# First norm in fewer steps, three start tiles on TensorE, norm tiles scaled ahead, and new places for the first chunks' second pieces

## The reference

```
def _modulate(h, shift, scale):
    return _rms(h) * (1.0 + scale) + shift

def _swiglu(h, w13, w2):
    a, b = jnp.split(h @ w13, 2, axis=-1)
    return (jax.nn.silu(a) * b) @ w2
...
    ml = _split_mod(cond_lat @ mod_w[i] + mod_b[i])
    mc = _split_mod(cond_ctx @ mod_w[i] + mod_b[i])
    h = h + 0.5 * ml[2] * _swiglu(_modulate(h, ml[0], ml[1]), ffn1_w13[i], ffn1_w2[i])
    hc = hc + 0.5 * mc[2] * _swiglu(_modulate(hc, mc[0], mc[1]), ffn1_w13[i], ffn1_w2[i])
```

## Time and profile before

| what | us |
|---|---|
| median of 3 runs | 1986.03 |
| lowest, highest | 1985.92, 1988.64 |
| profiled execution | 1990.15 |
| its span | 1988.5 |
| TensorE busy in it | 1927.3 |
| VectorE, ScalarE, GpSimd busy | 1149.1, 656.8, 156.7 |

### The profile page before, as it was taken

The page is one execution under the profiler, slowest core; times in us unless marked ns, Lnnn a source line. Parts: engine busy times, 40 slices in busy tenths (PEclk is TensorE's granted clock), DMA queues, the critical chain, the costliest instruction groups (busy, mean ns, idle before and its releaser), DMA issues.

```text
span 1988.5 us, 29548 instructions
## 1 busy us (share of the span) xinstructions
PE 1927.3 (97%) x11036; PEld 1695.6 (85%) x11036; DVE 1149.1 (58%) x1888; ACT 656.8 (33%) x1028; POOL 156.7 (8%) x212
## 2 busy tenths in 40 slices
PE   8899999999988899999999999999989999999998
PEld 7788888898965688888889888888888999999998
DVE  3887773345468558777533887752362532755554
ACT  2323222233236433322222423232243322544443
POOL 1210100100001211010010100100100000010000
PEclk9799999999989899999999999999999999999999
DMA  7365652234210036566332566633333220554554
GB/s 286 116 207 185 199 188 88 89 113 153 85 64 1 1 106 199 183 198 197 121 101 81 181 196 194 197 108 102 101 128 118 87 86 16 164 175 150 187 161 137
DMA packets 81004, 270.86 MB, mean 136 GB/s; under 512 B 8992, under 2 KB 14368, under 8 KB 80800
## 3 DMA queue, kind: packets, MB, share of 16 engines
q1 hardware_dynamic: 62496, 202.69, 31.3%
q0 software_dynamic: 18432, 67.12, 11.0%
HBM read 268.72 MB, written 1.05 MB: 136 GB/s over the span
## 4 chain that ended last, share of the span: by engine, by line
PE 91%; DVE 5%; issue 1%; ACT 1%; DMA 0%; POOL 0%; POOLq 0%; DVEq 0%; SPq 0%; ACTq 0%
PE pt L1167 22%; PE pt L1168 22%; PE pt L1170 22%; PE pt L1266 2%; PE pt L1375 2%; PE pt L1376 2%; PE pt L1374 2%; PE pt L1512 2%; PE pt L1514 2%; PE pt L1513 2%; PE pt L1458 1%; PE pt L1270 1%; DVE wl L735 1%; PE pt L1410 1%; PE pt L1391 1%
## 5 line engine op out<-in xcount | busy, mean ns | idle before, releaser
L735 DVE TENSOR_TENSOR wl<-raw,wh 128x1024 fp32r<-128x1024 f32 (+2 forms) x396 | 434.8, 1137 | 531.5 <-ACT wh L521 527.9
L1167 PE MATMUL pt<-xh,wh 128*128 128x512 f32 (+1 forms) x1648 | 595.0, 361 | 6.9 <-DVE wl L735 6.9
L1168 PE MATMUL pt<-xh,wl 128*128 128x512 f32 (+1 forms) x1648 | 594.0, 360 | 0.0
L1170 PE MATMUL pt<-xl,wh 128*128 128x512 f32 (+1 forms) x1648 | 592.2, 360 | 0.0
L521 ACT CAST wh<-raw 128x1024 fp32r<-128x1024 f32 (+2 forms) x396 | 366.0, 971 | 242.9 <-PE pt L1170 186.1
L1167 PEld LDWEIGHTS pt<-xh,wh 128*128 128x128 f32 x1648 | 313.0, 190 | 53.4 <-DVE wl L735 4.1
L1168 PEld LDWEIGHTS pt<-xh,wl 128*128 128x128 f32 x1648 | 312.9, 190 | 45.6
L1170 PEld LDWEIGHTS pt<-xl,wh 128*128 128x128 f32 x1648 | 312.7, 190 | 45.5
L747 DVE CUSTOM_DVE_ANT_0 pt<-modw,raw 128x1024 f32<-128x1024 f32 x256 | 305.7, 1256 | 5.0 <-DMA modw<-in_mod_rows 4.8
L1170 PE MATMUL pt<-ul,wh 128*128 128x512 f32 (+1 forms) x572 | 204.2, 357 | 0.0
L1167 PE MATMUL pt<-uh,wh 128*128 128x512 f32 (+1 forms) x572 | 204.2, 357 | 0.0
(11 more groups left out here) (169 smaller groups left out, 2355.3 us busy)
## 6 DMA issues: line engine op xcount, KB each, us to landing
raw<-in_ffn_w SPq DMA_DIRECT2D x240, 512.0 KB, 4.0
modw<-in_mod_rows POOLq DMA_DIRECT2D x128, 512.0 KB, 4.6
raw<-in_ret_w_in SPq DMA_DIRECT2D x48, 512.0 KB, 4.4
raw<-in_diff_w_in SPq DMA_DIRECT2D x24, 512.0 KB, 4.5
raw<-in_ffn_w SPq DMA_DIRECT2D x32, 256.0 KB, 3.9
raw<-in_ret_w_out SPq DMA_DIRECT2D x16, 512.0 KB, 4.2
region<-in_mod_start SPq DMA_DIRECT2D x9, 512.0 KB, 9.2
raw<-in_ffn_w SPq DMA_DIRECT2D x32, 128.0 KB, 3.4
```

Source lines behind the costliest of these rows:

```text
L735: nc.vector.tensor_tensor(flat(wl[:, s, cut]), raw[:, raw_slot(late, s, p), 0:part_rows * CW], flat(wh[:, s, cut].bitcast(F32)), ALU.subtr ...
L1167: nc.tensor.matmul(bank, wh[:, s, k, cut], hi(k), start=a, stop=False)
L1168: nc.tensor.matmul(bank, wl[:, s, k, cut], hi(k), start=False, stop=False)
L1170: return nc.tensor.matmul(bank, wh[:, s, k, cut], lo(k), start=False, stop=b)
```

## The change

There are four parts.

1. START_PE_SCALES is 3 instead of 1: TensorE makes the scale tiles of columns 0, 1 and 2, all ahead of the broadcast.
2. The second pieces of the first two chunks are loaded into the two modw slots. SyncE waits for nothing there, the pieces have semaphores of their own, ScalarE and VectorE read them from modw, and `raw_count` no longer counts the first pieces. GpSimd's first fetch into modw waits until both have been subtracted (lo_ready 4); it no longer stands behind any xl.
3. In norm 0 VectorE makes one scaled tile in two halves (hT times sc1 times the root), ScalarE adds the shift and rounds, and VectorE makes xl of tile k - 1 after the scaled tile of k (`start_lo`). GpSimd's xl step is gone, and tmp has four slots in turn.
4. In the later norms VectorE makes four scaled tiles (two in the second half) before the first xl, and keeps that lead. The two rests come at k = 0 and 2 (2 and 4). Ahead of ret_q the first copy_out with its cast, and the rest, stand before the second half's tiles; the second ones are at k = 3.

```diff
-START_PE_SCALES = 1
+START_PE_SCALES = 3
...
         def rests_among(ph):
-            return {4: {2: [(16, 0)], 4: [(16, 1)], DT: [(17, 0)], DT + 1: [(17, 1)]}, 2: {-1: [(9, 0), (9, 1)]},
-                    1: {4: [(5, 0)], 6: [(5, 1)]}}[len(ph["rows"])]
+            return {4: {0: [(16, 0)], 2: [(16, 1)], DT: [(17, 0)], DT + 1: [(17, 1)]}, 2: {-1: [(9, 0), (9, 1)]},
+                    1: {2: [(5, 0)], 4: [(5, 1)]}}[len(ph["rows"])]
...
             def start_pieces(p):
+
                 for s in range(2):
-                    if p:
-                        sp.wait_ge(lo_ready, s + 1)
-                    sp.dma_start(raw[:, s, :], column(w13[1][0], s * UP_PAIRS, p * DT // 2, DT // 2)).then_inc(raw_landed[s], 16)
+                    where = modw_slot[:, s] if p else raw[:, s, :]
+                    sp.dma_start(where, column(w13[1][0], s * UP_PAIRS, p * DT // 2, DT // 2)).then_inc(start_piece_landed[2 * p + s], 16)
...
-                    for k in range(DT):
-                        pool.wait_ge(affine, 2 * (k + 1))
-                        pool.wait_ge(x_hi_done, 2 * (k + 1))
-                        nc.gpsimd.tensor_tensor(xl[:, k, :], tmp[:, 2 + k % 2, :], xh[:, k, :].bitcast(F32),
-                                                ALU.subtract).then_inc(x_ready, 1)
...
+                    if u0 == START_UNITS:
+
+                        pool.wait_ge(lo_ready, 4)
...
-                                nc.scalar.activation(xh[:, k, cut], tmp[:, k % 2, cut], ACT.Identity, bias=modT[:, m0 + k, b:b + 1],
-                                                     scale=sc1[:, k, b:b + 1]).then_inc(x_hi_done, 1)
+                                nc.scalar.activation(xh[:, k, cut], tmp[:, k % 4, cut], ACT.Identity,
+                                                     bias=modT[:, k, b:b + 1]).then_inc(x_hi_done, 1)
...
+                        if after["kind"] == "ret_q":
+                            copy_out(after, qr, LAT, 0, 0)
                         for k in range(DT):
                             half_tile(1, k)
-                            if after["kind"] == "ret_q" and k % 4 == 3:
-                                copy_out(after, qr, LAT, 0, k // 4)
+                            if after["kind"] == "ret_q" and k == 3:
+                                copy_out(after, qr, LAT, 0, 1)
...
+                    def start_lo(k):
+                        for b in range(2):
+                            cut = slice(b * LAT, (b + 1) * LAT)
+                            dve.wait_ge(x_hi_done, 2 * k + b + 1)
+                            ins = nc.vector.scalar_tensor_tensor(xl[:, k, cut], tmp[:, k % 4, cut], modT[:, k, b:b + 1],
+                                                                 xh[:, k, cut].bitcast(F32), ALU.add, ALU.subtract)
+                        ins.then_inc(x_ready, 1)
...
-                        if k >= 2:
-                            dve.wait_ge(x_hi_done, 2 * (k - 1))
-                        nc.vector.tensor_tensor(tmp[:, k % 2, :], hT[:, k, :], pt[:, BC, :], ALU.mult).then_inc(normed, 1)
-                        dve.wait_ge(normed, k + 1)
-                        if k >= 2:
-                            dve.wait_ge(x_ready, k - 1)
+                        if k >= 4:
+                            dve.wait_ge(x_ready, k - 3)
                         for b in range(2):
                             cut = slice(b * LAT, (b + 1) * LAT)
-                            nc.vector.tensor_scalar(tmp[:, 2 + k % 2, cut], tmp[:, k % 2, cut], sc1[:, k, b:b + 1],
-                                                    modT[:, k, b:b + 1], ALU.mult, ALU.add).then_inc(affine, 1)
+                            ins = nc.vector.scalar_tensor_tensor(tmp[:, k % 4, cut], hT[:, k, cut], sc1[:, k, b:b + 1],
+                                                                 pt[:, BC, cut], ALU.mult, ALU.mult)
+                        ins.then_inc(normed, 1)
+                        if k:
+                            start_lo(k - 1)
+                    start_lo(DT - 1)
...
+                    for k in range(4):
+                        scaled_tile(0, k)
                     for k in range(DT):
                         rests(k)
-                        scaled_tile(0, k)
-                        if k:
-                            x_lo(0, k - 1)
-                    x_lo(0, DT - 1)
+                        x_lo(0, k)
+                        if k + 4 < DT:
+                            scaled_tile(0, k + 4)
...
+                        if after["kind"] == "ret_q":
+                            rest(2 * (after["q"] + 1), 0, late=is_late(after))
                         dve.wait_ge(bcast_ready, ph["st"] + 2)
+                        for k in range(2):
+                            scaled_tile(1, k)
                         for k in range(DT):
```

More of the change, by code:

```diff
@@ L263, in trunk @@
         x_hi_done = sem("x_hi_done")
-        normed, affine = sem("normed"), sem("affine")
+        normed = sem("normed")
         sq_ready, sq_added = sem("sq_ready"), sem("sq_added")
@@ L273, in trunk @@
         x_landed = [sem(f"x_landed{g}") for g in range(4)]
+        start_piece_landed = [sem(f"start_piece_landed{n}") for n in range(4)]
         start_made, start_step, start_cols = sem("start_made"), sem("start_step"), sem("start_cols")
@@ L359, in raw_count @@
             if not late:
-                return 2 * pair + s + 1
-            return pair - late_pair + 1 + (2 * late_pair if s == 0 else 0)
+                return 2 * pair + s - 1
+            return pair - late_pair + 1 + (2 * late_pair - 2 if s == 0 else 0)
         def is_late(ph):
@@ L561, in start_pieces @@
                 for s in range(2):
-                    act.wait_ge(raw_landed[s], 16 * (p + 1))
-                    nc.scalar.copy(flat(wh[:, s, p * DT // 2:(p + 1) * DT // 2]), raw[:, s, :]).then_inc(hi_ready, 1)
+                    cut = slice(p * DT // 2, (p + 1) * DT // 2)
+                    act.wait_ge(start_piece_landed[2 * p + s], 16)
+                    nc.scalar.copy(flat(wh[:, s, cut]), modw_slot[:, s] if p else raw[:, s, :]).then_inc(hi_ready, 1)
             act.wait_ge(cols_landed, 16)
@@ L741, in start_pieces @@
                     dve.wait_ge(hi_ready, 2 * p + s + 1)
-                    nc.vector.tensor_tensor(flat(wl[:, s, cut]), raw[:, s, :], flat(wh[:, s, cut].bitcast(F32)),
-                                            ALU.subtract).then_inc(lo_ready, 1)
+                    nc.vector.tensor_tensor(flat(wl[:, s, cut]), modw_slot[:, s] if p else raw[:, s, :],
+                                            flat(wh[:, s, cut].bitcast(F32)), ALU.subtract).then_inc(lo_ready, 1)
             def column_sum(dst, weights, j, products):
@@ L946, in _ @@
                     if T == TOK:
+                        if after["kind"] == "ret_q":
+                            rest(2 * (after["q"] + 1), 0, late=is_late(after))
                         dve.wait_ge(bcast_ready, ph["st"] + 2)
+                        for k in range(2):
+                            scaled_tile(1, k)
                         for k in range(DT):
-                            scaled_tile(1, k)
-                            if k:
-                                x_lo(1, k - 1)
-                            if k == DT - 1:
-                                x_lo(1, k)
-                            if after["kind"] == "ret_q" and k % 4 == 3:
-                                rest(2 * (after["q"] + 1) + k // 4, k // 4, late=is_late(after))
+                            x_lo(1, k)
+                            if k + 2 < DT:
+                                scaled_tile(1, k + 2)
+                            if after["kind"] == "ret_q" and k == 3:
+                                rest(2 * (after["q"] + 1) + 1, 1, late=is_late(after))
                     if units_of(L, first + 2) <= ph["unit"] - START_UNITS:
```

## The result

The changed kernel takes 2001.94 us (median of 4 runs, 1999.85 to 2005.69), against 1987.34 for the kernel before (4 runs, 1985.92 to 1990.4). The medians differ by 14.6 us. The ratio is 1.0068, 95% interval 1.0052 to 1.0084, which of 1987.34 is 13.5 us, 10 to 17: slower. The forecast was 1996.4, range 1986 to 2006, slower with 0.78.

A forecast was written before the change was run, and what follows sets the result against it. TensorE was taken to bound the kernel, so only its waits in the start and norms count. Start +21.7 and norms -11.3 gave +10.4, put on 1986.0 rather than the profiled 1990.15: 1996.4 us, range 1986 to 2006.

The forecast's parts named there:

- The head, +7.0: Start: two more scale tiles ahead of the broadcast delay S1, the end of column 1's shift tile on TensorE, by 7.0 us.
- S1 to S3, +0.4: Start, from column 1's shift tile end to column 3's: first turn unchanged, second 5.0 us against 4.56, so +0.4.
- S3 to S7, +13.3: Start, shift tile ends of columns 3 to 7: TensorE and VectorE take turns, three of four at 1.2 GHz, 40.0 us, +13.3.
- S7 to the end, +1.0: Start, from column 7's shift tile end to the last product: -0.5 at the high clock, +2.6 at the low, taken as +1.0.
- Behind it nothing changes: Behind the start: cast, small part and first loop pair follow the start's end as before, so no further change.
- The norms, -11.3: Later norms: 4.65 from three norms at 1.55 each, 0.25 at 722, 3.94 and 2.5 at ret_q; bounds -14.5 to -6.
- 1.37 plus the 0.51 of the pause in front: Norms at 417, 1085 and 1452: these TensorE waits go, less 0.3 for the moved piece, some 1.55 us each.
- The norm at 722: Norm with one chunk: moving both rests two tiles ahead shifts its 2.0 us of pauses rather than removing them, gaining 0.25.
- ret_q: Behind the norm at 1452: TensorE's 3.94 us wait for the next chunk's small part goes, and the high clock gives 2.5.
- (1): Start: the clock stays high or falls no more than before, +1.9 in all, 1987.9 us, no change told; chance 0.14.
- (2): Start: memory path freed of GpSimd decides, VectorE's sums set the old turn, -8.2 with the norms, 1977.8 us; chance 0.08.
- (3): Norms give nothing because the rests at k = 0 hold up xl: +21.7, 2007.7 us; chance 0.06.

The follow-up runs named there:

- e11: The kernel before with part 1 alone, three scale tiles on TensorE ahead of the broadcast: 1996.71 us, ratio 1.0036 to the kernel before.
- e4: The changed kernel with xl of tile k made right behind its scaled tile, ahead of the columns of k+1: 1986.05 us, ratio 0.9981 to the kernel before.
- e1: The kernel before with part 4 (the norms) alone: 1978.47 us, ratio 0.995 to the kernel before.
- e10: The kernel before with part 2 (second pieces loaded into modw) alone: 1990.72 us against 1990.33, ratio 0.9998.
- e2: The changed kernel without part 4, so only the start is changed: 2010.22 us, ratio 1.0107 to the kernel before.
- e3: The changed kernel with START_PE_SCALES back at 1: 2000.32 us, ratio 1.0058 to the kernel before.
- e7: The changed kernel with xl before the next columns, START_PE_SCALES 1, and an unused GpSimd subtraction beside columns 1 to 7: 1983.2 us, 4.1 over the same without it.
- e8: The changed kernel with START_PE_SCALES 1, second pieces handled at column 2, and xl of k between the two sums of column k+1: 1969.18 us, ratio 0.9904.
- e9: The changed kernel with START_PE_SCALES 1, second pieces handled at column 2, and xl of k ahead of both sums of column k+1: 1975.93 us, ratio 0.994.

## Why the prediction was right, point by point

**The head, +7.0: right.** S1 is 36.30 + 3.41 = 39.71 for a forecast of 39.2. 0.64 of it stands ahead of the change (20.81 against 20.17), so the two tiles cost 39.71 - 32.25 - 0.64 = 6.8; alone, in e11, 7.

**S1 to S3, +0.4: right.** S3 is 51.36: 11.65 from S1, against 43.48 - 32.25 = 11.23.

**S3 to S7, +13.3: the mechanism right, the share of the low clock a little too small.** S7 is 92.59, so 41.2 for a forecast of 40.0, +14.5. The turn at the low clock measures 9.87 (estimated 9.74) and the one at the high clock 7.44 (7.39). I took three of four low; the turns measure 8.3, 13.2 with the pieces (9.8 without), 9.9 and 9.9, so three low and one half so. The step that failed slightly is "I take three turns of four low". That part of the sum was an interpolation of the mean clock of before, not something read from a row. e4 shows the cause: with the order of xl undone the turn goes, and the low clock with it but for the pieces' column.

The Trainium skill ("TensorE: Matmul & The Clock Gate", Part 1: The HAM clock gate) says that the slow clock is the default and that activity releases it. The trace agrees in direction: in S3 to S7 TensorE was busy for 32.46 of 41.30 us, where it had been 23.14 of 26.70, and 0.58 was granted for 0.81. It does not bear the rule out at the head of the start, where TensorE worked without a pause from 20.81 to 39.7 us and its small tiles kept their 3.41 us.

**S7 to the end, +1.0: mis-sized.** 8.5 us for 9.9 forecast: the clock came back at 95 us, inside this stretch. Start in all: 101.09 - 79.09 = +22.0 for +21.7, with the 0.64 in it.

**"Behind it nothing changes": wrong for the profiled run, by -2.8 us.** The table of offsets begins with 19.17, not 22.0, and the rows place all of it: the first product behind the start is 22.00 us late (103.86 for 81.86), the fifteenth 19.18 (107.15 for 87.97). The first loop pair ran at 0.62 before and at 1.00 after. I checked its work and its waits, not its clock. But this is not the change's doing alone. e1, whose start is that of the kernel before, runs the same pair at the high clock; timeline of TensorE, the kernel before and then e1:

```profile
81.86 0.79 PE L1167 MATMUL pt<-xh,wh 128*128 128x512 f32 x1 [2.77 <-DVE wl L735]
82.44 0.63 PE L1168 MATMUL pt<-xh,wl 128*128 128x512 f32 x1
```
```profile
81.22 0.49 PE L1172 MATMUL pt<-xh,wh 128*128 128x512 f32 x1 [2.77 <-DVE wl L737]
81.56 0.40 PE L1173 MATMUL pt<-xh,wl 128*128 128x512 f32 x1
```

So this start can be left at either clock (in e10's profile, whose start differs only by part 2, it is left at the low one, as before), and the -2.8 is there only against a run that left it at the low one.

**The norms, -11.3: right in sign, too large.** The three norms gave 0.96, 0.96 and 0.98 us, not 1.55. The step that failed is "1.37 plus the 0.51 of the pause in front": it takes both waits as going to nothing. 0.46 and 0.28 of them stay (before: the earlier trace rows). In VectorE's rows an xl and the scaled tile behind it take 0.92 (443.12 to 444.04) in the first half, and 0.79 (1490.70 to 1491.49) in the second. In the first half the lead is four tiles, so the scaled tile takes the slot of the xl just ahead of it and has to wait for its end; in the second the lead is two. Four such pairs make 0.5 of the 0.59 that each norm fell short, and the sum closes: VectorE's two idle times of 1.31 and 0.18 went, less 0.5, is the 0.97 by which its hT step comes sooner behind the broadcast (9.99 us for 10.96). That is a reading of the rows and the code; no run tested it. The norm at 722 gave 0 for 0.25: its waits, 0.94 and 0.93, are now 1.07 and 1.08. ret_q gave 6.5 for 3.94 + 2.5 = 6.44: 15.87 to 9.36 in the table. 4.1 of it is there at the first product of the pair (1490.53 for 1478.77) and the other 2.4, the clock, 24 products later. Together -9.4; the loops between drifted by another 0.4.

**The sum and the level.** 22.0 - 2.8 - 9.4 - 0.4 is 9.4, for a span of +9.3 and a forecast of +10.4. That the forecast came within 1 us of the two profiled runs is in part luck, since its errors compensate: the norms were taken 1.9 too large, and the first pair's -2.8 was absent. The median missed by 5.5 because I took the 4.1 us between profiled run and median as a property that the change would leave. The runs of before, all those beside the experiments included, lie at two levels: with a granted clock of 0.985 or 0.986 they take 1985.3 to 1986.9, with one of 0.983 they take 1990.3 to 1992.1, and few lie between. The profiled one was of the second; the median of the first three runs was of the first. e1's profiled run has a mean clock of 0.986, and beside the profiled run of before it is 0.64 us ahead where the first loop pair starts and 3.4 at its fifteenth product (84.54 for 87.97) and at the broadcast of the next norm (416.89 for 420.33). So, if e1's run stands for the faster level, 3.4 of the some 5 us between the levels lie in the start and the first pair, and the profiles of the changed kernel, e2 and e3 all have that pair at the high clock. Counted from e1's start in place of the slower one's, the measured terms are 22.6 (103.86 for 81.22) - 9.4 - 0.4 = 12.8, and on the lower level that is 1998.8: 2.4 of the 5.5 us. The rest is that the four runs after took 1999.85 to 2005.69, which was not traced; the profiled one is the first of these, with a clock of 0.98 for 0.977 to 0.979.

**The range.** Its lower end takes 13 us for the norms where the bound given above it is 14.5; with that it is 1984.7 and not 1986. The result lies inside either way.

**The signs.** The broadcast ended at 36.5, S1 is 39.7, the start ended at 101.09, and ret_q's second pair waits for nothing, all as stated. The products' waits from tile 2 on are 2.60, 4.31, 0.96, 0.96 and 1.32 us, for some 1 to 3. The loops between moved by 0.4 us, where nothing was to move.

**Rivals.** (1), a clock no lower than before, is out: 0.58 for 0.81. (2), GpSimd's contention decides: out as what decides, but its mechanism is real, 4.1 us in e7. (3) is out by e1.

## What to carry to other kernels

Before taking steps away from a chain between two engines, write down for each step which of the other engine's results stands ahead of it in program order; a step moved behind the next round's wait can turn two engines that ran side by side into two that take turns, and here no saving on the steps made up for it. When such a loop is put right, fill the remaining waits with the next round's work that is already ready, since here the loop without pauses gained the clock as well as the pauses. Cost a change by the places where the pace-setting engine waits, and then read the clock of the stretch behind it too.

## What the runs showed of the hardware

A pause costs more than itself. In the start the order of xl costs 2.4 us a period in waiting and 2.4 in clock; e8 removes 3.4 us of TensorE's waits (1.47, 0.45, 0.32, 0.44 and 0.72 in the trace of e9) and gains 6.8. The spell at the low clock reaches into what follows: the first thirteen products behind the start took 0.63 us or more in the profiled run of the kernel before, and 0.39 or 0.40 in the changed one but for the first. The same start can end in either: in e1, which has it unchanged, they took the same 0.39 or 0.40.

The two-pass tiles of two columns kept TensorE busy from 20.81 to 39.7 us without the clock rising: 3.41 a tile throughout, 1.84 once the 512-column products had run. The granted clock of the profile read 1.00 for 30 to 52 us in the changed kernel although the tile at 36.30 took 3.41; durations, not the column, told it there.

A GpSimd step with two inputs of 128x512 and a VectorE sum of 1024 elements hold each other up, 2.2 us for the one (1.27 alone) and 2.3 for the other (1.22 alone), yet the VectorE sum in which GpSimd's step starts takes its normal time and the next one carries the delay. This is so in all seven columns of e7 and in columns 3, 4, 5 and 7 of the kernel before.

The kernel before has two levels of time, some 5 us apart, that go with a mean granted clock of 0.983 or of 0.985 to 0.986; e4 (11 runs within 2.5 us) and e8 (5 within 1.6) have one. Its own profile is of the slower level. Beside it, e1's profile, with the same start and the clock of the faster one, shows 3.4 us of the difference by the end of the first loop pair, 2.8 of them in that pair, run at 1.2 GHz in the one and at 2.4 GHz in the other. What decides between them was not shown.
